# Expert weights laid out with eight neighbouring contraction rows per partition, in a fused Mamba-2 and mixture-of-experts layer

## What is computed

```
gate, up = jnp.split(xb @ w_up[e], 2, axis=-1)      # xb: 128 x 1024, w_up[e]: 1024 x 2048
return (jax.nn.silu(gate) * up) @ w_down[e]         # w_down[e]: 1024 x 1024
```

## Time and profile before

| | us |
|---|---|
| median of 3 runs | 1214.65 |
| lowest, highest | 1210.5, 1215.7 |
| the profiled execution | 1218.35 |
| its span, first to last instruction | 1216.4 |
| PE busy in the span | 1022.0 (84%) |
| DVE busy | 934.6 (77%) |
| ACT busy | 645.8 (53%) |
| POOL busy | 461.6 (38%) |
| data moved | 289.04 MB, 238 GB/s on the mean |

### The profile page before, as it was taken

How to read it: one execution, slowest core, us unless ns; L and a number is a source line. 1 busy time by engine, 2 the same in 40 slices (tenths; PEclk the granted TensorE clock), 3 DMA queues, 4 the chain that set the end, 5 groups by cost and what they waited for, 6 DMA issues and landing times.

```text
span 1216.4 us, 15701 instructions
## 1 busy us (share of the span) xinstructions
PE 1022.0 (84%) x5222; PEld 844.1 (69%) x5222; DVE 934.6 (77%) x985; ACT 645.8 (53%) x599; POOL 461.6 (38%) x313
## 2 busy tenths in 40 slices
PE   0468999989998995853899999999999999999960
PEld 0447778867976974753677887777887778777740
DVE  4586994796599388785598888878888888888848
ACT  0144454345245334141577777667777767767641
POOL 0052554554364355511244422444223444224115
PEclk9988999998999998865899999999999999999985
DMA  4624532532351346043589999999999999999962
GB/s 142 245 87 150 162 88 87 153 106 69 121 169 55 97 145 207 1 175 121 225 336 367 365 373 374 374 353 359 360 381 372 386 361 364 360 365 375 357 206 110
DMA packets 105337, 289.04 MB, mean 238 GB/s; under 512 B 10193, under 2 KB 59481, under 8 KB 87901
## 3 DMA queue, kind: packets, MB, share of 16 engines
q1 hardware_dynamic: 99838, 268.77, 60.0%
q0 software_dynamic: 4752, 17.30, 5.4%
q10 hardware_dynamic: 720, 2.62, 0.5%
HBM read 272.94 MB, written 15.73 MB: 237 GB/s over the span
## 4 chain that ended last, share of the span: by engine, by line
DVE 22%; DMA 21%; PE 12%; issue 7%; ACT 6%; POOL 1%; DVEq 0%; ACTq 0%; SPq 0%; POOLq 0%
DMA moe<-in_moe_w_up 12%; DVE moe_r L1118 9%; DMA moe<-in_moe_w_down 8%; ACT moe_r L749 5%; PE ps L1548 2%; PE ps L1550 2%; PE ps L1552 2%; DVE moe L1210 1%; PE ps L1481 1%; DVE ssd L902 1%; PE ps L1506 1%; PE ps L1483 1%; PE ps L1482 1%; DVE moe_r L1204 1%; DVE ssd L885 1%
## 5 line engine op out<-in xcount | busy, mean ns | idle before, releaser
L1118 DVE TENSOR_TENSOR moe_r<-moe,moe_r 128x2048 fp32r<-128x2048 f32 x192 | 439.1, 2304 | 91.4 <-ACT moe_r L749 89.2
L749 ACT ACTIVATE moe_r<-moe 128x2048 fp32r<-128x2048 f32 x192 | 366.6, 1920 | 155.5 <-DMA moe<-in_moe_w_up 113.0
L1548 PE MATMUL ps<-moe_r 128*128 128x512 f32 x768 | 226.0, 403 | 11.9 <-DVE moe_r L1118 11.3
L1550 PE MATMUL ps<-moe_r 128*128 128x512 f32 x768 | 218.8, 394 | 0.0
L1552 PE MATMUL ps<-moe_r 128*128 128x512 f32 x768 | 216.4, 390 | 0.0
L448 POOL TENSOR_TENSOR ssd_r<-ssd,ssd_r 128x1024 fp32r<-128x1024 f32 x56 | 138.1, 2467 | 155.5 <-ACT ssd_r L592 155.3
L1548 PEld LDWEIGHTS ps<-moe_r 128*128 128x128 f32 x768 | 140.1, 190 | 47.9 <-DVE moe_r L1118 21.6
L1550 PEld LDWEIGHTS ps<-moe_r 128*128 128x128 f32 x768 | 145.9, 190 | 31.6
L1552 PEld LDWEIGHTS ps<-moe_r 128*128 128x128 f32 x768 | 145.0, 189 | 30.8
L544 POOL DMA_INDIRECT ysum<-moe,moe_i x16 | 32.3, 2018 | 330.7 <-ACT moe L781 304.9
L1336 PE MATMUL ps<-ssd_r 128*128 128x512 f32 x320 | 132.4, 414 | 18.1 <-DVE ssd L875 16.3
(11 more groups left out here) (246 smaller groups left out, 1456.0 us busy)
## 6 DMA issues: line engine op xcount, KB each, us to landing
moe<-in_moe_w_up SPq DMA_DIRECT2D x128, 1024.0 KB, 6.8
moe<-in_moe_w_down SPq DMA_DIRECT2D x64, 1024.0 KB, 7.0
ssd<-in_ssd_w_in SPq DMA_DIRECT2D x40, 512.0 KB, 4.0
ssd<-in_ada_w SPq DMA_DIRECT2D x32, 512.0 KB, 3.8
ssd<-in_ada_w SPq DMA_DIRECT2D x8, 1024.0 KB, 11.8
ssd<-in_ssd_w_out SPq DMA_DIRECT2D x16, 512.0 KB, 3.5
both<-in_x SPq DMA_DIRECT2D x4, 512.0 KB, 15.1
ysum<-both ACTq DMA_DIRECT2D x4, 512.0 KB, 4.7
```

The costliest lines, as they stand in the source:

```text
L749: act.activation(wr[:, i % RING, 0, :], ring[:, i % RING, :], ACT.Identity).then_inc(s_wh, 1)
L1118: dve.tensor_tensor(wr[:, i % RING, 1, :], ring[:, i % RING, :], wr[:, i % RING, 0, :].bitcast(F32), ALU.subtract).then_inc(s_wl, 1)
L1548: mm(to[i], xh, wh[i], start=start, stop=False)
L1550: mm(to[i], xh, wl[i], start=False, stop=False)
```

## The change

The 1024 contraction rows are dealt to partitions in another order. Before, piece k holds rows 128k + p for the partitions p; now it holds rows 8p + k. The left operands must follow, so the k-th transpose reads columns k, k+8, k+16, ... of `xg` or `hid`. Every eighth column comes from both halves of `hid`, so the first four transposes of `turn_hidden` now wait for both halves, and the wait ahead of the other four is gone.

```diff
-            up_v = w_up.rearrange("l e (k p) n -> (l e) p k n", p=P)
-            dn_v = w_down.rearrange("l e (k p) n -> (l e) p k n", p=P)
+            up_v = w_up.rearrange("l e (p k) n -> (l e) p k n", p=P)
+            dn_v = w_down.rearrange("l e (p k) n -> (l e) p k n", p=P)
...
-                        d = 4 * j + k
-                        op = nc.tensor.transpose(ps[:, 4 + j, k * P:(k + 1) * P], xg[:, d * P:(d + 1) * P], ident)
+                        op = nc.tensor.transpose(ps[:, 4 + j, k * P:(k + 1) * P], xg.rearrange("s (p k) -> s k p", k=DC)[:, 4 * j + k, :], ident)
...
-                    pe.wait_ge(s_hid, 2 * n + j + 3)
+                    if j == 0:
+                        pe.wait_ge(s_hid, 2 * n + 4)
                     for k in range(4):
-                        d = 4 * j + k
-                        op = nc.tensor.transpose(ps[:, 4 + j, k * P:(k + 1) * P], hid[:, d * P:(d + 1) * P], ident)
+                        op = nc.tensor.transpose(ps[:, 4 + j, k * P:(k + 1) * P], hid.rearrange("s (p k) -> s k p", k=DC)[:, 4 * j + k, :], ident)
```

## The result

| | before | changed kernel |
|---|---|---|
| median us, 16 runs each | 1215.95 | 1225.05 |
| lowest, highest | 1210.5, 1222.95 | 1214.91, 1230.21 |
| profiled execution's span, us | 1216.4 | 1228.3 |

The ratio is 1.0064, with a 95% interval of 1.0043 to 1.0085: the changed kernel is slower by some 8 us (the two medians lie 9.1 us apart). I had forecast 1211.5, 0.3% faster. The profiled execution of the changed kernel took 1230.21 us, the longest of its 16, so the differences between the two profiles overstate the loss.

A forecast was written before the change was run, and what follows sets the result against it. Loads, TensorE and POOL were taken as limits within some 5% of each other. From the profiled 1218.35 us, -3.6 (up), 0 (down), 0 (transposes) and +0.4 (last block) made 1215.15, as a median 1211.5, range 1202 to 1235.

The forecast's parts named there:

- The up loads, -3.6 us: w_up loads in the expert loop: strided form 2.5% faster, on their 144 us of the chain, saving 3.6 us.
- Its bound on this side, 13 us: Largest loss allowed for the w_up loads: 4% of 128 pieces at 2.56 us, 13 us.
- A gain cut off: Expert loop: loads, TensorE and POOL limit within some 5% of each other, so the next soon cuts off a gain.
- The down loads, 0: w_down loads in the loop: 8 KB runs instead of 4 KB gain nothing, 1.6 us either way.
- The transposes, 0: Transposes of xg and hid on TensorE: strided weight loads cost 0, upper bound 26 us if the load doubled.
- The rival on the strided weight load: TensorE in turn_rows and turn_hidden: slower strided weight loads add 19.7 us, giving 1231; chance 0.25.
- The wait in the last block, +0.4 us: Last block's hid transposes start later, waiting for both DVE halves: +0.4 us, bounds 0 and 0.64.
- The distance of 64 KB slows the loads: Rival on loop loads: up and down pieces take 4% longer, 9.2 us, giving 1224; chance 0.12.
- ACT's wait for up pieces falls: Sign in the loop's profile: this wait falls from 107.8 us by no more than 15.
- the thirteen turns shrink to some 476 us: Sign in the loop's profile: thirteen turns together take some 476 us, from 479.50 before.
- the shortest turn stays near what TensorE needs: Sign in the loop's profile: the shortest turn is still 34.9 us, with growth proving the prediction wrong.
- The sign of 418 GB/s: Loop stretches with only up pieces in flight should move 418 GB/s or more, from 409 to 411.

The follow-up runs named there:

- l2_up: Only w_up's new row order and the strided transposes of xg, loop raised to 64 blocks, against l0_before: 3020.74 us, +27.1.
- l5_uploads: Only the w_up loads in the new form, transposes as before (products pair wrong rows), 64 blocks, against l0_before: 3024.03 us, +30.4.
- the 16 KB form: Kernel before with w_up dealt two neighbouring rows to a partition, 8 KB runs 16 KB apart, transposes of xg to match: 1226.3 us, ratio 1.0071.
- 32 KB: Kernel before with w_up dealt four neighbouring rows to a partition, runs 32 KB apart, transposes of xg to match: 1220.45 us, ratio 1.0026.
- the down part alone: Kernel before with only w_down in the new order, strided transposes of hid and one wait for both halves: 1215.62 us, ratio 0.9993.
- l0_before: Kernel before with 64 blocks in the loop instead of 16, added blocks without tokens: 2993.61 us.

## Why the prediction was wrong, point by point

- **The up loads, -3.6 us.** This is the step that failed. Its sign was wrong: the runs with 64 blocks put it at +6.8 (l2_up) to +7.6 us (l5_uploads) for 16 blocks, of a total of some 8. I took the 2.5% between two stretches of in_ada_w and two of up pieces as the gain of the form, and applied it to the chain of the whole turn. The form has no such gain: alone, 24 pieces take 52.0 us instead of 52.1, and in the first 8 us behind `turn_rows` the loop moves 400 GB/s instead of 403. The 409 and 411 GB/s of the earlier trace rows were stretches near the top of a turn whose means run from 274 to 403. And the turn has a stretch at the start of the scatter where the form moves 4% less. The prediction mentioned that the in_ada_w stretches have no gather beside them and drew from it only that nothing would be gained. Its bound on this side, 13 us, held.
- **A gain cut off.** I had written that loads, TensorE and POOL stand close and a gain in one is cut off by the next, and then counted the whole chain's share. The long runs fit the warning, with TensorE idle for 17 us more ahead of `slot_rows` in 2200 us, but do not show that POOL is what cuts the gain off.
- **The down loads, 0.** Held: 1215.62 against 1215.8 us, and -3.4 us over 64 blocks.
- **The transposes, 0.** Nearly held: 0.86 us for eight instead of 0.82, 1.3 us over all 32 groups, where the bound of a doubled load was 26 and the rival's price 19.7. The rival on the strided weight load falls with it. The Trainium skill's rule on SBUF cachelines ("SBUF — State Buffer", under "Door 1: The DMA port swizzle"), by which every read in a new line pays, fits the longer duration of the single load, but the pace hardly changes, as the last section shows. That the lines are the reason was not tested.
- **The wait in the last block, +0.4 us.** Held: 2.24 - 1.74 makes 0.5 us, and the transposes run without a gap behind the second half.
- **The rivals.** "The distance of 64 KB slows the loads", 1224 with a chance of 0.12, named the right transfer and nearly the right time (1225.05), with the wrong mechanism, so that its number is luck: there is no slow distance as such, as loads alone show at 64 KB, and the 16 KB form, which loses as much. It also charged the down pieces, which lose nothing. The rule of the Trainium skill beside it ("DMA: Bandwidth & Descriptors", "Latency and other measured facts") tells of pitches of 512 KiB and more; no run here shows those.
- **The signs named beforehand.** That ACT's wait for up pieces falls and that the thirteen turns shrink to some 476 us failed in the first profile (116.4 and 488.4 us), and that the shortest turn stays near what TensorE needs could not tell. The sign of 418 GB/s in stretches with only up pieces, and of the distance being to blame below 400, was a bad one: single stretches of the changed kernel lie on both sides (424 at 854 to 862 us, 352 at 861 to 867), and only means over many turns tell, in which kernels with the old form lie below 400 too (369 from 12 to 18 us).

What stays open: how the form of a plain load and the indirect DMAs act on each other, what makes the other three quarters of the 0.48 us, and whether 32 KB really loses less than 16 KB. The spread of the rows' addresses against the eight 1 MB stretches of an expert was not varied. No run has the scatter without the gather; the windows point at the scatter, whose packets run first, from 20 to 25 us behind `turn_rows`. No version beat the kernel before; the down part alone (0.9993) is the same.

## What to carry to other kernels

A load's rate that was read where nothing else is in flight holds for such stretches only, and two short stretches are too few to take 2.5% from; cut the turn into stretches by what is in flight, and price a new memory form in each, above all beside indirect transfers. Where three limits stand within a few per cent of each other, count a gain only up to the next one's wait. Before a wait is named as the cause, look whether it grows in a variant that loses nothing. If single executions scatter by more than the effect, lengthen the loop: four times the blocks turned an unclear part (1.0066, with a profile that spoke against it) into 27 us, some six times the standard error of a difference between two kernels with four runs each, with means of sixty turns behind them.

## What the hardware showed that I had not expected

- **Strided weight loads.** The weight load of a transpose reads 128 columns that now lie 32 bytes apart. By the groups of TensorE's loads in the changed kernel:

```profile
L1540 PEld LDWEIGHTS ps<-both,moe 128*128 128x128 f32 x128 | 16.7, 192 | 3.0 <-DVE moe L1210 1.8
L1531 PEld LDWEIGHTS ps<-both,moe 128*128 128x128 f32 x128 | 16.4, 194 | 4.7 <-issue 2.7 <-DMA moe<-h2d,moe_i 1.3
```

  The same loads in the kernel before:

```profile
L1541 PEld LDWEIGHTS ps<-both,moe 128*128 128x128 f32 x128 | 14.8, 140 | 2.8 <-DVE moe L1210 0.9
L1532 PEld LDWEIGHTS ps<-both,moe 128*128 128x128 f32 x128 | 14.8, 145 | 5.3 <-issue 3.4 <-DMA moe<-h2d,moe_i 1.2
```

  Each takes 192 to 194 ns on the mean instead of 140 to 145. Yet eight in a row pass in 0.86 us instead of 0.82. Eight times 192 ns would be 1.54 us, so they overlap: the duration of one is no measure of the pace.
- **Pieces in flight.** Loads of 1 MB in 8 KB runs need 52 us from the first issue to the 24th at four in flight and 58 to 71 us at two. At two in flight the run that is one stretch of memory was the uneven one (62.0 and 71.3 us), the one 64 KB apart steady (57.9 and 59.4), in two stretches each.
- **Run length.** Runs of 4 KB cost 54.0 us where 8 KB cost 52.1, alone, and 0.5% of the kernel's time when all up pieces had them, while the kernel could not tell 4 KB from 8 KB runs in its down pieces, though alone these took 53.6 and 52.0 us.
- **An accumulating scatter.** From 20 to 24 us behind `turn_rows` in l0_before, a 4 KB packet of the scatter takes 327 ns, and one of the gather, from 26 us on, 159 ns. Beside the scatter the core's rate is down to 296 GB/s (22 to 24 us), beside the gather it is 409 (26 to 28 us). So of the two it is the scatter that costs the loads their rate.
